# The first transfers of a two-layer encoder kernel in another order, with the rotary angles, sines and tables made behind the first products

## What is computed

```
u    = RMSNorm(x) * g_mix_pre
proj = u @ w_in        -> q, k, v of attention A | cq | ckv and k_pe | two gates
A    : windowed attention, 16 heads of 64, rotary on all 64 dimensions, with sinks
B    : latent attention; cq = RMSNorm(cq) @ w_uq, ckv = RMSNorm(ckv) @ w_ukv, rotary on 32 dimensions
x    = x + RMSNorm((sigmoid(gate_A) * (yA @ w_oa) + sigmoid(gate_B) * (yB @ w_ob)) @ w_out)
x    = x + RMSNorm(relu(RMSNorm(x) @ w_mlp_in)^2 @ w_mlp_out)
```

## Time and profile before

| | us |
|---|---|
| median of 3 runs | 827.09 (827.08 to 827.15) |
| the profiled execution | 826.92 |
| its span, first to last instruction | 825.0 |
| TensorE busy | 803.2 (97%) |
| VectorE busy | 509.8 (62%) |
| ScalarE busy | 408.0 (49%) |
| POOL busy | 125.2 (15%) |

### The profile page before, as it was taken

The page is one execution under the profiler, slowest core; times in us unless marked ns, Lnnn a source line. Parts: engine busy times, 40 slices in busy tenths (PEclk is TensorE's granted clock), DMA queues, the critical chain, the costliest instruction groups (busy, mean ns, idle before and its releaser), DMA issues.

```text
span 825.0 us, 12057 instructions
## 1 busy us (share of the span) xinstructions
PE 803.2 (97%) x4613; PEld 696.4 (84%) x4613; DVE 509.8 (62%) x685; ACT 408.0 (49%) x747; POOL 125.2 (15%) x204
## 2 busy tenths in 40 slices
PE   6999999999999999999989999999999999999997
PEld 5987878888779999999879788788878899999995
DVE  5768766575785555545566877566576844555554
ACT  5757434444474444444466574444346654444452
POOL 2443000001231000000114420000031200000000
PEclk9999999999999999999999999999999999999999
DMA  7647422334636555565327482331436565565521
GB/s 236 234 159 265 166 71 85 102 102 153 203 115 224 180 186 170 196 203 191 97 72 267 160 297 80 102 102 54 151 126 209 176 201 171 189 200 173 186 103 51
DMA packets 68462, 132.21 MB, mean 160 GB/s; under 512 B 2842, under 2 KB 10564, under 8 KB 68164
## 3 DMA queue, kind: packets, MB, share of 16 engines
q1 hardware_dynamic: 68276, 131.12, 47.9%
q10 hardware_dynamic: 144, 0.52, 0.2%
HBM read 130.59 MB, written 1.05 MB: 160 GB/s over the span
## 4 chain that ended last, share of the span: by engine, by line
PE 92%; DVE 4%; ACT 3%; issue 0%; DMA 0%; POOLq 0%; ACTq 0%; POOL 0%; DVEq 0%
PE acc L1167 17%; PE acc L1169 17%; PE acc L1168 17%; PE sc L1417 7%; PE sc L1416 7%; PE sc L1415 7%; PE tp L1144 5%; PE acc L1283 5%; PE sc L1251 4%; PE acc L1201 4%; ACT s_hi L605 2%; DVE w_lo L853 1%; ACT w_hi L582 1%; PE sc L1167 1%; PE sc L1169 1%; PE sc L1168 1%
## 5 line engine op out<-in xcount | busy, mean ns | idle before, releaser
L853 DVE TENSOR_TENSOR w_lo<-raw,w_hi 128x1024 fp32r<-128x1024 f32 (+3 forms) x256 | 312.8, 1237 | 187.9 <-ACT w_hi L582 186.3
L582 ACT CAST w_hi<-raw 128x1024 fp32r<-128x1024 f32 (+3 forms) x256 | 252.3, 995 | 217.8 <-PE acc L1169 146.6
L1167 PE MATMUL acc<-w_hi,s_hi 128*128 128x512 f32 (+3 forms) x680 | 263.0, 387 | 3.7 <-DVE w_lo L853 3.7
L1168 PE MATMUL acc<-w_lo,s_hi 128*128 128x512 f32 (+3 forms) x680 | 257.6, 379 | 0.0
L1169 PE MATMUL acc<-w_hi,s_lo 128*128 128x512 f32 (+3 forms) x680 | 257.6, 379 | 0.0
L1167 PEld LDWEIGHTS acc<-w_hi,s_hi 128*128 128x128 f32 x680 | 127.9, 188 | 27.9 <-DVE w_lo L853 5.6
L1169 PEld LDWEIGHTS acc<-w_hi,s_lo 128*128 128x128 f32 x680 | 127.8, 188 | 24.0
L1168 PEld LDWEIGHTS acc<-w_lo,s_hi 128*128 128x128 f32 x680 | 128.0, 188 | 21.1
L1415 PE MATMUL sc<-s_hi,w_hi 128*128 128x256 f32 x448 | 126.9, 283 | 0.0
L1417 PE MATMUL sc<-s_hi,w_lo 128*128 128x256 f32 x448 | 126.8, 283 | 0.0
L1416 PE MATMUL sc<-s_lo,w_hi 128*128 128x256 f32 x448 | 126.8, 283 | 0.0
(11 more groups left out here) (143 smaller groups left out, 779.0 us busy)
## 6 DMA issues: line engine op xcount, KB each, us to landing
raw<-in_w_mlp_in SPq DMA_DIRECT2D x32, 1024.0 KB, 5.3
raw<-in_w_mlp_out SPq DMA_DIRECT2D x32, 1024.0 KB, 5.0
raw<-in_w_in SPq DMA_DIRECT2D x24, 1024.0 KB, 5.4
raw<-in_w_oa SPq DMA_DIRECT2D x8, 1024.0 KB, 5.0
raw<-in_w_out SPq DMA_DIRECT2D x8, 1024.0 KB, 5.0
raw<-in_w_ob SPq DMA_DIRECT2D x4, 1024.0 KB, 5.1
raw<-in_w_in SPq DMA_DIRECT2D x4, 768.0 KB, 4.6
raw<-in_w_in SPq DMA_DIRECT2D x4, 576.0 KB, 7.0
```

The costliest lines, as they stand in the source:

```text
L582: s.copy(split_view(w_hi, p), raw_view(p)).then_inc(hi_ready, 1)
L853: v.tensor_tensor(split_view(w_lo, p), raw_view(p), split_view(w_hi, p).bitcast(F32), ALU.subtract)\
L1167: mm(banks[t][:, 0:N], h[:, kk, tk], wh[:, k, :], start=(start and k == 0), stop=False)
L1168: mm(banks[t][:, 0:N], h[:, kk, tk], wl[:, k, :], start=False, stop=False)
```

## The change

SP's queue begins with x's first tile and goes on to the weights. The four lists of norm scales and the positions are started by ScalarE, as its first five instructions, ahead of x's second tile. VectorE makes the angles (`take_angles`) in layer 0 after the last `s_lo` of x and before `lo` of piece 4. ScalarE takes the two Sin and the one-column Exp (`take_sines`) in layer 0 after the cast of piece 10 and before the sums of squares of ckv. POOL makes the tables (`tables`) in layer 0 after the six reciprocal norms of x, cq and ckv. The instructions in them are the same; VectorE and POOL get a semaphore each for their chains of dependent steps.

```diff
         @block.sync
         def _(sp):
-            sp.dma_start(pos_i[:, :], pos_d[0].rearrange("(t p) -> p t", p=P),
-                         allow_slow_non_contiguous=True).then_inc(pos_loaded, 16)
             sp.dma_start(x[:, 0, :], x_d[0, 0:P, :]).then_inc(x_loaded[0], 16)
-            for src, (c, n) in zip((g_mix_pre, g_mlp_pre, q_norm, kv_norm), GAINS):
-                sp.dma_start(gain_rows[DEPTH * c:DEPTH * (c + n), :],
-                             src.rearrange("l (k p) -> (l k) p", p=P)).then_inc(gains_loaded, 16)
...
+                if l == 0:
+
+                    pool.wait_ge(rstd_ready, 3 * TT)
+                    tables()
...
-            act.wait_ge(angles, 1)
-            s.activation(sint[:, :, 1, :], ang[:, :, :], ACT.Sin).then_inc(sines, 1)
-            s.activation(turns[:, :, :], ang[:, :, :], ACT.Sin, scale=0.5).then_inc(sines, 1)
-
-
+            for src, (c, n) in zip((g_mix_pre, g_mlp_pre, q_norm, kv_norm), GAINS):
+                act.dma_start(gain_rows[DEPTH * c:DEPTH * (c + n), :],
+                              src.rearrange("l (k p) -> (l k) p", p=P)).then_inc(gains_loaded, 16)
+            act.dma_start(pos_i[:, :], pos_d[0].rearrange("(t p) -> p t", p=P),
+                          allow_slow_non_contiguous=True).then_inc(pos_loaded, 16)
             act.wait_ge(x_loaded[0], 16)
             act.dma_start(x[:, 1, :], x_d[0, P:2 * P, :]).then_inc(x_loaded[1], 16)
...
-            act.wait_ge(sines, 2)
-            s.activation(neg_m[:, 0:1], turns[:, 0, 0:1], ACT.Exp)
+            def take_sines():
+                act.wait_ge(angles, 1)
+                s.activation(sint[:, :, 1, :], ang[:, :, :], ACT.Sin).then_inc(sines, 1)
+                s.activation(turns[:, :, :], ang[:, :, :], ACT.Sin, scale=0.5).then_inc(sines, 1)
+                act.wait_ge(sines, 2)
+                s.activation(neg_m[:, 0:1], turns[:, 0, 0:1], ACT.Exp)
...
                 hi(pos, 10)
+                if l == 0:
+                    take_sines()
...
                 turned(pos, ("x", 1, 1))
+                if l == 0:
+                    take_angles()
```

More of the change, by code:

```diff
@@ L269, in build @@
         pool_step = sem("pool_step")
+        table_step = sem("table_step")
+        angle_step = sem("angle_step")
         act_step = sem("act_step")
@@ L462, in _ @@
                 pool.wait_ge(consts_ready, half + 1)
[L465 to L469, removed]
             def to_rstd(pos, name):
@@ L493, in square, with tables @@
                     g.tensor_tensor(tok[:, t, 0:COL], k_b[:, t, 0:COL], k_b[:, t, 0:COL], ALU.mult).then_inc(h_ready, 1)
+            def tables():
+                made = Steps(pool, table_step)
+                pool.wait_ge(sines, 2)
+                made.link(g.tensor_tensor(cost[:, :, :], turns[:, :, :], turns[:, :, :], ALU.mult))
+                made.link(g.tensor_scalar(cost[:, :, :], cost[:, :, :], -2.0, 1.0, ALU.mult, ALU.add))
+                g.tensor_scalar(sint[:, :, 0, :], sint[:, :, 1, :], -1.0, None, ALU.mult).then_inc(tables_ready, 1)
+                pool.wait_ge(tables_ready, 1)
             origin = steps.n
@@ L818, in _ @@
                 dve.sem_inc(x_ready[t], 2)
[L820 to L837, removed]
             steps.link(v.memset(gain_all[:, DEPTH, :], 0.0))
@@ L846, in _, with take_angles @@
             v.tensor_copy(gain[:, :], gain_all[:, 0, :]).then_inc(gains_now, 1)
+            def take_angles():
+                made = Steps(dve, angle_step)
+                dve.wait_ge(freq_ready, 1)
+                dve.wait_ge(pos_loaded, 16)
+                made.link(v.tensor_copy(pos_f[:, :], pos_i[:, :]))
+                for t in range(TT):
+                    ins = v.tensor_scalar(ang[:, t, :], freq[:, :], pos_f[:, t:t + 1], None, ALU.mult)
+                made.link(ins)
+                magic = 1.5 * 2.0 ** 23
+                two_pi = 2 * np.pi
+                c1 = 6.28125
+                c2 = float(np.floor((two_pi - c1) * 2 ** 20) / 2 ** 20)
+                c3 = float(two_pi - c1 - c2)
+                pi_in = 3.14159250259
+                made.link(v.tensor_scalar(turns[:, :, :], ang[:, :, :], 1.0 / two_pi, magic, ALU.mult, ALU.add))
+                made.link(v.tensor_scalar(turns[:, :, :], turns[:, :, :], magic, None, ALU.subtract))
+                for c in (c1, c2, c3):
+                    made.link(v.scalar_tensor_tensor(out=ang[:, :, :], in0=turns[:, :, :], scalar=-c, in1=ang[:, :, :],
+                                                      op0=ALU.mult, op1=ALU.add))
+                v.tensor_scalar(ang[:, :, :], ang[:, :, :], pi_in, -pi_in, ALU.min, ALU.max).then_inc(angles, 1)
             def lo(pos, upto):
```

## The result

The changed kernel takes 829.69 us (median of 8 runs, 828.57 to 831.27) against 826.97 (8 runs, 825.84 to 827.39): ratio 1.0039, interval 1.0029 to 1.0049. So it is slower: by 2.7 us from the medians, by 0.4% or 2.4 to 4.1 us from the ratio and its interval. The forecast was 1.1 slower, with a difference too small to be told from none as the likeliest of the three outcomes.

What follows compares the result with a forecast made beforehand. TensorE was taken as a pipe that starts late and is then full. First copy +0.17, angles +0.6 and sines +0.3 made +1.1 us: 828.0 profiled, 828.2 median, range 826.8 to 829.8.

Steps and rivals of the forecast that it cites:

- What bounds the kernel: TensorE starts late and is then full, without idle from 10.85 up to 33.41; a shifted start counts once, whole.
- The scales: Start: fourth scale list, issued by ScalarE at 2.07, lands at 4.7, between 4.3 and 7.5, against 5.33 before.
- rival 2: Start: scales slowed like x's second half, landing 6.2 to 7.5, start 1.7 to 3.0 us late, 829.7 to 831; 14%.
- The table load in front of the first copy: ScalarE, behind the transposes: load starts at 6.05, costs 1.30, so first copies at 7.35, 0.17 us later than before.
- Angles: VectorE, between x's last s_lo and piece 4's w_lo: 2.37 us of work, TensorE stops 0.6 us at piece 4.
- Sines: ScalarE, after piece 10's cast: 3.1 us of loads, Sin and Exp, TensorE waits 0.3 us for piece 11.
- Transfers of x and weights: Start: x some 0.5 us and first weights 2.1 us earlier, in by 6.1 at the latest; buys nothing.
- tables: POOL, three small operations behind the sums; their first users come later, so they cost nothing.
- layer 2: The later layer: unchanged by the edit.
- 1: Start: rival that the table load runs early, copies start before 6.3, 826.9 us; 20%, and 6% for 826.0.
- 3: ScalarE: rival that each table load costs about another 1.28 us from emptying the engine, 832.0 us; 5%.

Runs made afterwards that it cites:

- c3: Changed kernel with an early Exp table load, SP holding back all weights but the first load until the scales are in: 828.25 us, ratio 1.0013.
- b1: Changed kernel with SP's weights held back until all four scale lists are in: 829.04 us, ratio 1.0023.
- b3: Kernel before with only the changed kernel's first transfers; angles, sines, Exp and tables stay at the head: 831.88 us, ratio 1.0060.
- a3: Changed kernel with the scales back on SP behind x and an early Exp table load: 826.89 us, ratio 0.9999.
- b2: a3 with angles moved to right after the norm scales are read, sines and Exp to after piece 3's cast: 826.12 us, ratio 0.9991.
- c1: b2 with x's second tile issued by ScalarE only after the first cast: 825.38 us, ratio 0.9982.
- b4: b2 with two scale lists on SP behind x and the two small ones on ScalarE ahead of the positions: 826.79 us, ratio 0.9994.
- c2: b2 with 23 unread identity transposes on TensorE ahead of its first product: 825.62 us, ratio 0.9986.
- d1: b2 with both edits, c1's later second tile of x and c2's idle transposes: 825.17 us, ratio 0.9981.

## Why the prediction was wrong

- **What bounds the kernel**: right. The change plays in the first 38 us, and its loss there is handed to the end whole (4.15 us at piece 11, 4.2 at the end).
- **The scales**: this step failed, by its size. The prediction took 4.7 for the landing out of 4.3 to 7.5, "near the lower end, since the scales are 21 KB"; it was 7.36. It priced the weights beside the last list at 0.4 us over the 2.26 alone; they cost 2.8 (5.04 in all), and the issue was 0.25 later than taken (2.32, not 2.07). It had the right row for it, the second half of x with 3.2 us more in company, and set it aside for the size. Its other argument, that the scales are queued before most of the weights, doesn't help either: c3 shows 1.9 us of delay with one load beside them. From b1 to the changed kernel the weights cost a 1 KB transfer 4.8 us (2.3 to 7.1), the last list of 2 KB 2.7 (2.3 to 5.0) and one of 512 KB 3.4 (3.9, with weights issued 0.4 behind it, to 7.3 with four loads ahead): the delay is not in proportion to the size. This is 2.7 us of the difference between forecast and profile, and rival 2, at 14%, is what happened (landing in its 6.2 to 7.5, the median at its lower bound of 829.7).
- **The table load in front of the first copy**: right in place and price. Forecast 1.35 + 1.30 behind the landing, measured 1.43 + 1.30. With the late landing the first copies came at 10.09, beyond the 8.5 that the prediction had named as the sign of being wrong.
- **Angles**: the place was right, the stop 0.3 instead of 0.6. Their chain took 2.0 us (23.69 to 25.66) where it had taken 2.37 at the head: the pair that was L824 takes 0.39 instead of 0.71. It takes 0.39 at the head too in b3, where POOL has long finished its memsets, so the 0.71 goes with what stood beside it there (POOL's memset of `mask`, 3.06 to 3.80); no run takes that memset alone away (the two lines stand below).
- **Sines**: forecast 0.3, measured 0.4, to the step.
- **Transfers of x and weights, tables, layer 2**: nothing, as said. The first load landed at 6.5 (1.18 + 5.3), not by 6.1, long before its cast at 11.10; where the first copy is early (a3, b2), this landing does hold the first cast.
- **Left out altogether**: TensorE's pace in the first product, 0.6 us in the profile.
- Of the rivals, 1 was wrong at its condition (the load waits), 3 has no support: each load is followed by the next activation 1.30 after its start, with no drain on top.

The pair at L824 in the kernel before, then in b3:

```profile
3.14 0.71 DVE L824 TENSOR_SCALAR ang<-freq,pos_f 128x32 f32<-128x32 f32 x2
```

```profile
9.52 0.39 DVE L824 TENSOR_SCALAR ang<-freq,pos_f 128x32 f32<-128x32 f32 x2
```

With 7.36 in place of 4.7 the prediction's own sum is 1.1 + 2.7 = 3.8 us. The profiled execution lost 4.35: the pace adds 0.6, and the stop at piece 4 gives 0.3 back. The medians lost 2.7, so the corrected sum is 1.1 too much for them. The scales landed at 7.11 to 7.36 in all three traces with four loads beside them, so their landing is an unlikely place for that 1.1; it stays open. That the measured median still lies just inside the range (upper end 829.8) is no merit of the sum: its 828.2 is below all eight runs.

## What to carry to other kernels

Moving a small transfer that everything waits for to a second, empty queue buys issue time and can lose more than that, since the transfer shares its engines with what the first queue has already been given; put it ahead of the bulk on the same queue, and keep back bulk that isn't needed yet (c1: about 0.7 us for one line, of which the trace gives the start 0.3 and the pace the rest). Ahead of the bulk is no guarantee: in b4 a list there took 4.4 us. When the first activation of a kernel changes, look for where its table load comes to stand. Work that is moved off the start is only free where its engine idles: the same angles and sines made two stops of 0.7 us together behind the first products and none some 18 us earlier, in the engines' waits for data (b2).

## What the runs showed that I had not expected

- The granted clock is recorded as 1.00 in every stretch of the first 25 us, yet 384-column matmuls start 0.32 us apart at first and 0.17 to 0.18 later. By an estimate of one column a cycle, 0.32 is the lower level, 1.2 GHz, and 0.16 would be 2.4. So the record of the clock doesn't show this rise, and only the starts do. The same eight products (between the first product's hi*hi and the second tile's transposes) take 2.03 us in the kernel before, 2.56 in the changed one and 1.47 in a3, so the rise doesn't keep its place in the work. Idle transposes from 2.56 on brought it ahead of the first product (c2, d1). What else moves it from run to run is open.
- POOL's steps are three to five times as long beside VectorE's w_lo: the three table steps took 0.30, 0.24 and 0.38 at the head, and in the changed kernel, beside VectorE's w_lo (37.76 to 41.4), about 1.2 each (below). In b2 w_lo runs from 31.87 to 34.33 and again from 34.66: the second step, begun inside it, takes 1.10, the third, begun between the two, again 0.38. Here it cost nothing, since nobody waits for the tables until much later.
- Landing times at the start vary by half a microsecond between kernels with the same order of transfers (4.90 to 5.45 for the scales on SP), and whole runs of one kernel by 1.0 to 2.9 us, where three runs of before had agreed within 0.07.

```profile
37.99 1.15 POOL L489 TENSOR_TENSOR cost<-turns 128x64 f32<-128x64 f32 x1
39.23 1.10 POOL L490 TENSOR_SCALAR cost<-cost 128x64 f32<-128x64 f32 x1
40.41 1.22 POOL L491 TENSOR_SCALAR sint<-sint 128x64 f32<-128x64 f32 x1
```

and in b2:

```profile
33.33 1.10 POOL L493 TENSOR_SCALAR cost<-cost 128x64 f32<-128x64 f32 x1
34.51 0.38 POOL L494 TENSOR_SCALAR sint<-sint 128x64 f32<-128x64 f32 x1
```
